# The down product of the experts turned: weights held in 64-column blocks, rows of h streamed

## The reference, cut to what matters

```
combine = route(t, w_router, router_bias)                 # two experts per token
h = silu(einsum('td,edf->tef', t, w_gate)) * einsum('td,edf->tef', t, w_up)
y = einsum('tef,efd->td', h * combine[:, :, None], w_down)
```

## Time and profile before

| what | us |
|---|---|
| median of the runs | 1264.74 |
| profiled execution, its own time | 1262.56 |
| span of its trace | 1260.8 |
| PE busy | 1068.2 (85%) |
| PE busy in L851, L861, L873 | 179.3, 174.7, 227.4 |
| experts' stage of layer 0 (first gate product to end of last down product) | 500.29 to 786.34 |
| experts' stage of layer 1 | 915.89 to 1201.8 |

### The profile page before, as it was taken

How to read it: one execution, slowest core, us unless ns; L and a number is a source line. 1 busy time by engine, 2 the same in 40 slices (tenths; PEclk the granted TensorE clock), 3 DMA queues, 4 the chain that set the end, 5 groups by cost and what they waited for, 6 DMA issues and landing times.

```text
span 1260.8 us, 27022 instructions
## 1 busy us (share of the span) xinstructions
PE 1068.2 (85%) x11219; PEld 763.1 (61%) x11219; DVE 378.2 (30%) x792; ACT 200.1 (16%) x433; POOL 122.4 (10%) x189
## 2 busy tenths in 40 slices
PE   7899999899999961999999999198099999999910
PEld 6678878545544411777777776187077777777700
DVE  1334444233233233111111111694421111111155
ACT  1234444300222101000000000121020000000011
POOL 0001011120033003000000000430300000000042
PEclk9989999999799975999999999587599999999965
DMA  9324245110023186999999999424479999999541
GB/s 341 138 73 149 80 144 185 56 48 1 1 75 90 53 354 232 325 380 392 392 390 389 399 396 354 157 70 168 151 250 390 384 387 392 402 394 390 202 163 52
DMA packets 80859, 295.96 MB, mean 235 GB/s; under 512 B 10184, under 2 KB 41168, under 8 KB 72495
## 3 DMA queue, kind: packets, MB, share of 16 engines
q1 hardware_dynamic: 53351, 247.50, 52.5%
q10 hardware_dynamic: 19712, 26.75, 6.2%
q0 software_dynamic: 7760, 21.24, 5.1%
HBM read 255.80 MB, written 40.11 MB: 235 GB/s over the span
## 4 chain that ended last, share of the span: by engine, by line
PE 83%; DVE 7%; DMA 3%; POOL 2%; issue 2%; ACT 2%; ACTq 0%; SPq 0%; POOLq 0%; DVEq 0%
PE PS L873 18%; PE PS L851 14%; PE PS L861 13%; PE PS L781 6%; PE PS L569 4%; PE PS L730 4%; PE PS L631 3%; PE PS L616 3%; PE PS L753 2%; PE PS L711 2%; PE PS L786 2%; PE PS L525 2%; PE PS L827 2%; PE PS L547 2%; POOL expert_rows L992 1%
## 5 line engine op out<-in xcount | busy, mean ns | idle before, releaser
L873 PE MATMUL PS<-ring,arena 128*96 128x512 f32 x512 | 227.4, 597 | 0.0
L851 PE MATMUL PS<-arena,ring 128*64 128x96 f32 x4096 | 179.3, 249 | 51.7 <-DVE arena L1586 51.7
L851 PEld LDWEIGHTS PS<-arena,ring 128*64 128x64 f32 x4096 | 173.3, 139 | 75.7 <-issue 75.7
L861 PE MATMUL PS<-arena,ring 128*64 128x96 f32 x4096 | 174.7, 246 | 0.2 <-issue 0.2
L861 PEld LDWEIGHTS PS<-arena,ring 128*64 128x64 f32 x4096 | 171.0, 137 | 0.4 <-issue 0.4
L873 PEld LDWEIGHTS PS<-ring,arena 128*96 128x96 f32 x512 | 80.8, 163 | 123.0 <-issue 119.2
L1586 DVE STREAM_TRANSPOSE arena<-arena 128x768 uint32<-128x768 uint32 x34 | 54.2, 1593 | 205.4 <-ACT arena L1171 175.5
L1606 DVE COPY arena<-PS 96x512 f32<-96x512 f32 x32 | 22.0, 687 | 218.0 <-PE PS L873 218.0
L1175 ACT ACTIVATE arena<-PS 96x512 f32<-96x512 f32 x32 | 19.0, 593 | 379.8 <-PE PS L873 379.8
L1012 POOL DMA_INDIRECT arena<-expert_out,ids x20 | 20.2, 1012 | 599.0 <-DMA expert_out<-arena 589.0
L781 PE MATMUL PS<-ring,arena 128*128 128x512 f32 (+1 forms) x160 | 75.8, 636 | 1.3 <-issue 0.7
(11 more groups left out here) (225 smaller groups left out, 1059.7 us busy)
## 6 DMA issues: line engine op xcount, KB each, us to landing
ring<-w_gate SPq DMA_DIRECT2D x32, 2048.0 KB, 14.6
ring<-w_up SPq DMA_DIRECT2D x32, 2048.0 KB, 15.3
ring<-w_down SPq DMA_DIRECT2D x32, 2048.0 KB, 15.7
arena<-expert_rows ACTq DMA_DIRECT2D x144, 96.0 KB, 9.7
expert_out<-arena ACTq DMA_DIRECT2D x32, 384.0 KB, 7.8
expert_rows<-ring SPq DMA_DIRECT2D x6, 1920.0 KB, 10.0
ring<-cache_ckv SPq DMA_DIRECT2D x64, 128.0 KB, 2.0
ring<-w_o SPq DMA_DIRECT2D x1, 4096.0 KB, 19.1
```

The lines of the kernel that those rows point to most:

```text
L851: last = nc.tensor.matmul(bank(s, KF, CAP)[at:at + 64, f, :], wg[w][:, k, P * f + at:P * f + at + 64], xeT[s][:, k, :], start=(k == 0), st ...
L861: last = nc.tensor.matmul(out[at:at + 64, :], wu[w][:, k, P * f + at:P * f + at + 64], xeT[s][:, k, :], start=(k == 0), stop=(k == KD - 1))
L873: last = nc.tensor.matmul(bank(4 + hf)[0:CAP, :], h[s][:, f, :], wd[w][:, f, 512 * hf:512 * (hf + 1)], start=(f == 0), stop=(f == KF - 1))
```

## The change

The down product holds weights and streams `h`. For each of eight planes m and four blocks f, 128 columns of `wd` that lie 8 apart (8j + m) are held as two blocks of 64, and 96 rows of `h` are streamed. The result is turned: partition p of plane m has column 8p + m of the 96 rows, planes 0 to 3 in bank 4 and 4 to 7 in bank 5. Two stream transposes on DVE turn 32 x 32 blocks back into `ys`, now 32 partitions by 3 rows by 256 columns for each quarter of the width, and four DMAs of 1 KB pieces store them. ACT has no copy any more. `down_ps` counts two per tile, `y_st` 64.

```diff
-        ys = [view(arena, 5120 + 1024 * s, D) for s in range(2)]
+        ys = [view(arena, 5120 + 1024 * s, CAP // 32, D // 4) for s in range(2)]
...
-                    for blocks in (range(KF - 1), (KF - 1,)):
-                        if KF - 1 in blocks:
-                            pe.wait_ge(q["h_set"], 2 * tl + 2)
-                        for hf in range(2):
-                            for f in blocks:
-                                last = nc.tensor.matmul(bank(4 + hf)[0:CAP, :], h[s][:, f, :], wd[w][:, f, 512 * hf:512 * (hf + 1)],
-                                                        start=(f == 0), stop=(f == KF - 1))
-                    last.then_inc(q["down_ps"][s], 1)
+                    def down(m, blocks):
+                        for f in blocks:
+                            eighth = wd[w][:, f, :].rearrange("p (a m) -> p m a", m=KD)[:, m, :]
+                            for at in (0, 64):
+                                last = nc.tensor.matmul(bank(4 + m // 4, 4, CAP)[at:at + 64, m % 4, :], eighth[:, at:at + 64],
+                                                        h[s][:, f, :], start=(f == 0), stop=(f == KF - 1))
+                        return last
+                    down(0, range(KF - 1))
+                    down(4, range(KF - 1))
+                    pe.wait_ge(q["h_set"], 2 * tl + 2)
+                    down(0, (KF - 1,))
+                    down(4, (KF - 1,))
+                    for m in (1, 2, 3, 5, 6, 7):
+                        last = down(m, range(KF))
+                        if m in (3, 7):
+                            last.then_inc(q["down_ps"][s], 1)
...
-                    nc.scalar.activation(ys[s][0:CAP, 0:512], bank(4)[0:CAP, :], ACT.Copy).then_inc(q["y_set"], 1)
                     act.wait_ge(q["y_set"], 2 * tl + 4)
-                    act.dma_start(yd[bass.ds(CAP * tl, CAP), :], ys[s][0:CAP, :]).then_inc(q["y_st"][s], 16)
+                    for c in range(4):
+                        act.dma_start(yd[bass.ds(CAP * tl, CAP), 256 * c:256 * (c + 1)].rearrange("(a j) d -> j a d", j=32),
+                                      ys[s][32 * c:32 * (c + 1), :, :]).then_inc(q["y_st"][s], 16)
...
-                    v.tensor_copy(ys[s][0:CAP, 512:D], bank(5)[0:CAP, :]).then_inc(q["y_set"], 1)
+                    for g in range(2):
+                        dve.wait_ge(q["down_ps"][s], 2 * u + g + 1)
+                        v.transpose(ys[s].rearrange("p a (i m) -> p a m i", m=KD)[:, :, 4 * g:4 * g + 4, :].bitcast(mybir.dt.uint32),
+                                    bank(4 + g, 4, CAP).rearrange("p m (a j) -> p a m j", j=32).bitcast(mybir.dt.uint32)
+                                    ).then_inc(q["y_set"], 1)
```

More of the change, by code:

```diff
@@ L460, in _ @@
                 else:
-                    load_expert(1, 0, 1, (S[0]["gate_ps"][0], nh), (S[0]["up_ps"][0], 2 * nh), (S[0]["down_ps"][0], nh))
+                    load_expert(1, 0, 1, (S[0]["gate_ps"][0], nh), (S[0]["up_ps"][0], 2 * nh), (S[0]["down_ps"][0], 2 * nh))
                     sp.wait_ge(S[0]["xeT_set"], 2 * nh + 1)
@@ L470, in _ @@
                     sp.dma_start(t["o_pool_s"][0, :, CTX - 1, :], X[0:DB, 4, :]).then_inc(pool_out, 16)
-                    load_expert(1, 1, 0, (S[0]["gate_ps"][1], nh), (S[0]["up_ps"][1], 2 * nh), (S[0]["down_ps"][1], nh))
+                    load_expert(1, 1, 0, (S[0]["gate_ps"][1], nh), (S[0]["up_ps"][1], 2 * nh), (S[0]["down_ps"][1], 2 * nh))
                 sp.wait_ge(tab_set, 2 * L + 2)
@@ L477, in _ @@
                         ex = sp.value_load(tile_ids[0:1, bass.ds(2 * u + s, 1)], min_val=0, max_val=E - 1)
-                        load_expert(L, ex, 1 - s, (q["gate_ps"][s], u), (q["up_ps"][s], 2 * u), (q["down_ps"][s], u))
+                        load_expert(L, ex, 1 - s, (q["gate_ps"][s], u), (q["up_ps"][s], 2 * u), (q["down_ps"][s], 2 * u))
             for i in range(4):
@@ L1004, in _ @@
                 for s in range(2):
-                    hold(pool_e, q["y_st"][s], 16 * nh)
+                    hold(pool_e, q["y_st"][s], 64 * nh)
                 def gather(i):
@@ L1154, in experts @@
                 nh = act.value_load(n_half[0:1, 0:1], min_val=E // 2, max_val=TILES // 2)
-                act.sem_inc(q["y_set"], 1)
                 act.wait_ge(scat, 160 * (L + 1))
@@ L1162, in experts, with tile @@
                     nc.scalar.activation(X[0:n, i, :], X[0:n, i, :], ACT.Copy, scale=ALPHA).then_inc(xscaled, 1)
-                def tile(u, s, stored):
+                def tile(u, s):
                     tl = 2 * u + s
@@ L1171, in tile @@
                     nc.scalar.activation(sg[s], bank(s, KF, CAP), ACT.Silu).then_inc(q["sg_set"], 1)
-                    act.wait_ge(q["down_ps"][s], u + 1)
-                    if stored:
-                        act.wait_ge(q["y_st"][s], 16 * u)
-                    nc.scalar.activation(ys[s][0:CAP, 0:512], bank(4)[0:CAP, :], ACT.Copy).then_inc(q["y_set"], 1)
                     act.wait_ge(q["y_set"], 2 * tl + 4)
-                    act.dma_start(yd[bass.ds(CAP * tl, CAP), :], ys[s][0:CAP, :]).then_inc(q["y_st"][s], 16)
[L1179 to L1183, removed]
+                    for c in range(4):
+                        act.dma_start(yd[bass.ds(CAP * tl, CAP), 256 * c:256 * (c + 1)].rearrange("(a j) d -> j a d", j=32),
+                                      ys[s][32 * c:32 * (c + 1), :, :]).then_inc(q["y_st"][s], 16)
+                with act.Fori(0, nh) as u:
+                    tile(u, 0)
+                    tile(u, 1)
             def take_pages(b):
@@ L1582, in experts @@
                 nh = dve.value_load(n_half[0:1, 0:1], min_val=E // 2, max_val=TILES // 2)
-                dve.sem_inc(q["y_set"], 1)
+                dve.sem_inc(q["y_set"], 2)
                 def turn_rows(s):
@@ L1602, in tile @@
                     v.tensor_tensor(h[s][:, KF - 1, :], sg[s][:, KF - 1, :], bank(6 + s, CAP), ALU.mult).then_inc(q["h_set"], 1)
-                    dve.wait_ge(q["down_ps"][s], u + 1)
                     if stored:
-                        dve.wait_ge(q["y_st"][s], 16 * u)
-                    v.tensor_copy(ys[s][0:CAP, 512:D], bank(5)[0:CAP, :]).then_inc(q["y_set"], 1)
+                        dve.wait_ge(q["y_st"][s], 64 * u)
+                    for g in range(2):
[3 more added lines that the diff above has]
+                                    ).then_inc(q["y_set"], 1)
                 tile(0, 0, False)
```

## The result

| | us |
|---|---|
| before, median of 4 runs beside it | 1265.55 (1263.69 to 1272.49) |
| after, median of 4 runs | 1284.00 (1277.56 to 1291.38) |
| ratio | 1.0137, 95% interval 1.0071 to 1.0204 |
| after, profiled execution | 1284.12, span 1282.4 |

The change made the kernel slower by 1.4%, 18 us, where I had forecast 1245 us; the third rival, weights at half speed in the open, said 1288 us at 120 ns. I follow the profiled executions: the span grew from 1260.8 to 1282.4 us, by 21.6.

What follows compares the result with a forecast made beforehand. PE set the end with DMA equally full and slightly behind, so PE's gain would become waiting for weights. Layer 1 -11.2 and layer 0 -7.0 make -18.2 us: 1244.4 us profiled, stated as 1245; range 1234 to 1300, own case 1234 to 1252.

Steps and rivals of the forecast that it cites:

- the third rival, weights at half speed in the open: Down product: held columns 8 apart outlast the stream; 1333 us at 142 ns, 1288 at 120; chance 0.22.
- the 2.2 us that it names: Whole kernel: the profiled execution lay 2.2 us below its runs' median; forecast stated as 1245 us after 1244.4.
- Price of the held columns: Down product: columns 8 apart load as quickly as neighbours, 5.28 us a tile instead of 7.04.
- My two-sided bound from the earlier trace: Down product at half-speed weight loads: 64 x 111 ns = 7.1 us to 64 x 142 ns = 9.1 us.
- DMA as a floor: Expert stages: DMA needs 18.23 us a tile, PE 15.99, so PE's gain turns into waiting for weights.
- Row loads, "wanted more than a whole tile after their issue": ACT's queue: four store issues, about 2 us, ahead of the next row loads do no harm.
- +0.25 us a tile: DMA: extra cost of storing 384 pieces of 1 KB instead of 96 of 4 KB, between 0 and 0.44.
- Transposes: DVE's second transpose of 384 elements: 0.80 us, between 0.52 and 1.6; the first runs under planes 4 to 7.
- Tail of layer 1: After layer 1's last down product: second transpose and four store issues for one add 1.1 us (0.5 to 2.4).
- ACT and DVE hidden: Per tile ACT loses 0.59 us of work and DVE gains 0.9; busy 1.1 and 3.0 of 17.75, hidden.
- Layer 0's give-back: After layer 0's stage: 5.3 of the 12.3 us gained return to transfers formerly hidden, leaving -7.0 us.
- Clock: PE's gate product: a lower clock costs 1.9 us more, fits into DMA's 18.2 and doesn't change the sum.

Runs made afterwards that it cites:

- experiment 3: Changed kernel with one store of 128 pieces of 3 KB: 1260.09 us (ratio 0.9978) with neighbouring held columns, 1278.88 us (1.0120) with columns 8 apart.
- experiment 4: Changed kernel with neighbouring held columns and its four stores issued on POOL's queue instead of ACT's: 1253.93 us, ratio 0.9927.
- experiment 1: Changed kernel with the 64 held columns of w_down next to each other, all else the same: 1270.58 us, ratio 1.0059.
- experiment 5: Changed kernel with neighbouring held columns, eight PE transposes replacing DVE's, ACT and DVE copies, one store of 4 KB rows: 1257.37 us, ratio 0.9957.

## Why the prediction was wrong

The forecast of 1245 us and the 1284.00 measured are 39 us apart. The kernels of experiment 3 part this into 18.8 us for the distance of the held columns, 5.1 for the small stores (less sure, as said), and 15.1 for a gain that was not there with neighbours and large pieces either. (By its own sum the forecast would be 1246.6: 1244.4 and the 2.2 us that it names.)

- **Price of the held columns** (the step that failed: 18.8 us, and with it the sign). I took the lower end, 5.28 us, "of all rows that of L861 is nearest, in form and count". Measured 7.79. My two-sided bound from the earlier trace rows, 7.1 to 9.1 at half speed, held it, and so did the rival with its point of decision at 110 ns: 122 ns per half was measured, and the rival gave 1288 us for 120 where 1284.0 was measured. The mistake was to call L861 the nearest row because of its shape, when the one property that the change altered, the distance, was just what L861 doesn't have; the row that had it, DVE's transpose, was slow, and I put that down to transposing. The argument that a weight load takes "half of what the stream takes", so that a slower read has room, failed too: the stream takes 82.5 / 96 = 0.86 ns a column per half, as long as the 0.87 of a weight load and not twice as long. 64 columns 8 apart needed 122 ns per half where 82.5 were free.
- **DMA as a floor.** The mechanism was right, and it comes as soon as PE is fast (experiments 3 and 4), but not in the change, where PE is slower than the floor. The size was off: 18.4 to 19.0 us a tile instead of 18.23. The large gain was never there: of the forecast's 18 us experiments 3 and 4 show 3 and 9.
- **Row loads, "wanted more than a whole tile after their issue".** The second step that failed. I summed engine time of the small pieces (+0.25 us a tile) and not turns; the queue's landing went from 9.7 to 16.1 us in the change and to 20.2 with a fast PE. With the columns' price taken away, these late rows still leave a loss (experiment 1, +0.6%). I had also missed that `state_pool` waits for the last of them: forecast at 789.2, it landed at 799.7 in experiment 3.
- **Transposes** were sized well: 0.88 us each for 0.80. **Tail of layer 1**: +0.6 for +1.1. **ACT and DVE hidden**: yes, although ACT now loads its table 16 times for the silu (L1179, 20.5 us in all), where the kernel before did it twice (L1171). That comes with the missing copy (experiment 5, with copies on ACT again, has two), but the cause isn't tested by itself; ACT is off the chain and it costs nothing here.
- **Layer 0's give-back** of 5.3 us could not show where the stage lost time instead. In experiment 4 it is 4.5 of 7.7 us, in experiment 3 all of the 5.9 that the stage had gained.
- **Clock**: 1.00, the upper level, in all four windows of after, and without weight in the sum, as said. Where PE waits for rows it has weight: in experiment 1 it adds 1.9 us to the down product behind a wait of 3.1 us, on the chain.

Open: what share of the 18 us the two stalls have in an average run; why PE stands still in early tiles of experiment 5; why 64 bytes apart (207 ns) are a little cheaper than 32 (218); how large the floor's gain by 8 KB pieces is, as no kernel had it without another bound. Pairs of columns, held in the order 0, 1, 16, 17, would give two hits per 16 bytes and keep the rows' order; this was not tried and nothing here shows what it would give.

## What to carry to other kernels

Where an operand's distance in SBUF changes, look for the price in a row that has that distance, not in one that has the same shape, and take the slower end until one run says otherwise: a held block with fewer than two float32 in 16 bytes cost 80 ns more per 64 columns. Where a transfer gets smaller pieces, count the packets on its queue against those of the busiest queue beside it: in these runs the row loads came late from a quotient of about one on, and bytes or engine time didn't show it. When one engine is made faster, ask for the landings of every load that has slack now, the small ones too.

## What the runs showed of the hardware that I had not expected

- Weight loads of 64 float32 columns take 137 to 138 ns at 4 and 8 bytes apart and 207 to 218 ns at 16, 32 and 64 bytes: a step, not a slope.
- The same store calls were moved in 384 packets of 1 KB a tile by ACT's queue and in 128 of 3 KB by POOL's (91615 and 83423 packets in all). With packets of 3 KB on both, the stores cost 0.5% more on ACT's queue, ahead of the row loads, than on POOL's (1260.09 and 1253.93 us).
- Behind a wait of 3.1 us for `h` PE ran at a granted clock of 0.76 in the mean of the next 7.17 us, and the down product took 1.9 us more (experiment 1).
- Larger packets on one queue slowed another: with 8 KB for 4 KB pieces of `w_down`, the row loads on ACT's queue went from 12.6 to 18.3 us.
